# One matmul granule later for the first down product of an F part, and the projection's weights ahead of the last eight expert granules

## The reference

```python
def swiglu(v, wg, wu, wd):
    return (jax.nn.silu(v @ wg) * (v @ wu)) @ wd

def moe_swiglu(v, router, wg, wu, wd):
    ...
    y = jnp.zeros_like(v)
    for e in range(N_EXPERTS):                      # 8 experts, F = 2816
        y = y + combine[..., e:e + 1] * swiglu(v, wg[e], wu[e], wd[e])
    return y
...
    h = h + moe_swiglu(v, moe_router[j], moe_wg[j], moe_wu[j], moe_wd[j])
    ple_g = jax.nn.sigmoid((rmsnorm(h, norm_ple[i]) @ ple_gate[i]).astype(F32)).astype(h.dtype)
    h = h + ple_g * (p[i] @ ple_proj[i])
return rmsnorm(h, norm_final)
```

## Time and profile before

| | |
|---|---|
| median of 3 runs | 1570.85 us (1567.13 to 1571.53) |
| profiled execution, its own time | 1569.91 us |
| its span on the core | 1568.2 us |
| PE busy | 1537.9 us (98% of the span) |
| DVE, ACT, POOL busy | 600.8, 465.2, 63.2 us |
| read from HBM | 413.23 MB, 267 GB/s over the span |

### The profile page before, as it was taken

How to read it: one execution, slowest core, us unless ns; L and a number is a source line. 1 busy time by engine, 2 the same in 40 slices (tenths; PEclk the granted TensorE clock), 3 DMA queues, 4 the chain that set the end, 5 groups by cost and what they waited for, 6 DMA issues and landing times.

```text
span 1568.2 us, 33642 instructions
## 1 busy us (share of the span) xinstructions
PE 1537.9 (98%) x15282; PEld 1181.6 (75%) x15282; DVE 600.8 (38%) x831; ACT 465.2 (30%) x659; POOL 63.2 (4%) x101
## 2 busy tenths in 40 slices
PE   8999999999999999999999999999999999999987
PEld 7887888888888888788867677677766767777666
DVE  5787878555556777788210000000000000000025
ACT  5656434544455556434300000000000001000024
POOL 3100000000000100000000000000000000001001
PEclk9999999999999999999999999999999999999999
DMA  8445446565555445454999999999999999999940
GB/s 294 145 151 162 157 140 195 188 193 188 188 189 170 146 160 163 135 183 168 364 354 393 394 353 409 344 408 382 372 407 341 409 355 394 394 357 409 396 145 28
DMA packets 163396, 420.31 MB, mean 268 GB/s; under 512 B 16818, under 2 KB 42212, under 8 KB 163252
## 3 DMA queue, kind: packets, MB, share of 16 engines
q1 hardware_dynamic: 159168, 407.69, 71.6%
q0 software_dynamic: 2432, 8.65, 1.6%
q10 hardware_dynamic: 1652, 1.80, 0.4%
HBM read 413.23 MB, written 4.85 MB: 267 GB/s over the span
## 4 chain that ended last, share of the span: by engine, by line
PE 97%; ACT 1%; DVE 1%; DMA 0%; POOL 0%; issue 0%; SPq 0%; POOLq 0%; ACTq 0%; DVEq 0%
PE ps L2018 42%; PE ps L1561 15%; PE ps L1563 14%; PE ps L1562 14%; PE ps L2059 2%; PE ps L1660 1%; PE ps L2085 1%; PE ps L1621 1%; PE ps L1807 1%; PE ps L1670 1%; ACT ffT_area L634 1%; DMA arena<-in_w_in 0%; PE ps L2088 0%; PE ps L2095 0%; PE ps L2009 0%; PE ps L1831 0%
## 5 line engine op out<-in xcount | busy, mean ns | idle before, releaser
L1561 PE MATMUL ps<-whi,ahi 128*128 128x512 f32 (+1 forms) x984 | 391.2, 398 | 4.6 <-DVE wlo L982 3.0
L1563 PE MATMUL ps<-wlo,ahi 128*128 128x512 f32 (+1 forms) x984 | 383.2, 389 | 0.0
L1562 PE MATMUL ps<-whi,alo 128*128 128x512 f32 (+1 forms) x984 | 382.6, 389 | 0.0
L982 DVE TENSOR_TENSOR wlo<-arena,whi 128x1024 fp32r<-128x1024 f32 (+1 forms) x246 | 289.0, 1217 | 83.9 <-ACT whi L634 83.0
L634 ACT ACTIVATE whi<-arena 128x1024 fp32r<-128x1024 f32 (+1 forms) x246 | 245.6, 1053 | 99.9 <-PE ps L1563 89.1
L1476 DVE TENSOR_TENSOR ff_area<-ff_area,ps 128x768 f32<-128x768 f32 x24 | 22.9, 954 | 642.4 <-PE ps L2018 642.4
L2018 PE MATMUL ps<-arena 128*32 128x512 f32 (+3 forms) x3816 | 267.1, 428 | 0.0
L2018 PEld LDWEIGHTS ps<-arena 128*32 128x32 f32 x3816 | 188.8, 110 | 63.7 <-issue 1.3
L1561 PEld LDWEIGHTS ps<-whi,ahi 128*128 128x128 f32 x984 | 184.9, 188 | 47.3 <-issue 9.0
L2018 PE MATMUL ps<-expert_ring,arena 128*32 128x256 f32 (+3 forms) x3096 | 217.1, 426 | 0.0
L1563 PEld LDWEIGHTS ps<-wlo,ahi 128*128 128x128 f32 x984 | 184.7, 188 | 38.9
(11 more groups left out here) (260 smaller groups left out, 920.0 us busy)
## 6 DMA issues: line engine op xcount, KB each, us to landing
arena<-in_w_in SPq DMA_DIRECT2D x112, 512.0 KB, 4.5
arena<-in_moe_wd SPq DMA_DIRECT2D x92, 512.0 KB, 7.5
expert_ring<-in_moe_wd SPq DMA_DIRECT2D x84, 512.0 KB, 7.5
arena<-in_moe_wu SPq DMA_DIRECT2D x76, 512.0 KB, 9.0
arena<-in_moe_wg SPq DMA_DIRECT2D x68, 512.0 KB, 8.5
expert_ring<-in_moe_wg SPq DMA_DIRECT2D x60, 512.0 KB, 8.3
expert_ring<-in_moe_wu SPq DMA_DIRECT2D x52, 512.0 KB, 9.9
arena<-in_moe_wu SPq DMA_DIRECT2D x36, 384.0 KB, 3.9
```

The source lines that it names most:

```text
L982: return V.tensor_tensor(dst, src, hi.bitcast(f32), ALU.subtract)
L1561: TE.matmul(o, ahi[:, sa], whi[:, sw], start=start, stop=False)
L1562: TE.matmul(o, alo[:, sa], whi[:, sw], start=False, stop=False)
L1563: return TE.matmul(o, ahi[:, sa], wlo[:, sw], start=False, stop=stop)
```

## The change

It has three parts. First, in the lists for parts 1 and 2, D0 and D4 stand one place later: behind g1.2 and g2.2. Second, the loads of ple0, ple1 and ple2 stand in SP's order ahead of those of the last eight expert granules (u2.1 to D10 of the last expert); these eight lie in `arena` alone, and since three of its seven slots now hold the ple weights, they share the other four. So `RING_DONE` falls to 272. Third, ACT and DVE split these three granules at the places of u2.2, u2.3 and D6 of the last expert, where before they did it at the end of the expert and, for the last one on DVE, after it.

```diff
@@ -55,9 +55,9 @@
-MOE_ORDER += [("gate", 1, 0), ("gate", 1, 1), ("down", 0, 0), ("gate", 1, 2), ("gate", 1, 3), ("down", 1, 0), ("up", 1, 0),
+MOE_ORDER += [("gate", 1, 0), ("gate", 1, 1), ("gate", 1, 2), ("down", 0, 0), ("gate", 1, 3), ("down", 1, 0), ("up", 1, 0),
               ("up", 1, 1), ("down", 2, 0), ("up", 1, 2), ("up", 1, 3), ("down", 3, 0)]
-MOE_ORDER += [("gate", 2, 0), ("gate", 2, 1), ("down", 4, 0), ("gate", 2, 2), ("gate", 2, 3), ("down", 5, 0), ("up", 2, 0),
+MOE_ORDER += [("gate", 2, 0), ("gate", 2, 1), ("gate", 2, 2), ("down", 4, 0), ("gate", 2, 3), ("down", 5, 0), ("up", 2, 0),
               ("up", 2, 1), ("up", 2, 2), ("up", 2, 3)]
@@ -76,14 +76,19 @@
-SLOT_OF = [FREED[m % len(FREED)] for m in range(N_MOE)]
-for part in range(5):
-    waiting = [m for m in range(len(SLOT_OF)) if SLOT_OF[m] < ARENA_SLOTS and SLOT_OF[m] not in SLOT_OF[m + 1:]]
-    SLOT_OF.append(SLOT_OF[waiting[0]])
-BEFORE = [max([k for k in range(m) if SLOT_OF[k] == SLOT_OF[m]], default=None) for m in range(len(SLOT_OF))]
-USE = [sum(SLOT_OF[k] == SLOT_OF[m] for k in range(m)) for m in range(len(SLOT_OF))]
-RING_DONE = max(m for m in range(N_MOE) if SLOT_OF[m] >= ARENA_SLOTS) + 1
-OVER_SLOT = [slot for slot in range(ARENA_SLOTS) if slot not in SLOT_OF[N_MOE:]][0]
+TAIL = 8
+LOADS = list(range(N_MOE - TAIL)) + [N_MOE + i for i in range(3)] + list(range(N_MOE - TAIL, N_MOE)) + [N_MOE + 3, N_MOE + 4]
+SLOT_OF, BEFORE, USE, held = {}, {}, {}, {slot: [] for slot in FREED}
+for at, m in enumerate(LOADS):
+    if at < len(FREED):
+        slot = FREED[at]
+    else:
+        free = [slot for slot in FREED if held[slot][-1] < N_MOE and (slot < ARENA_SLOTS or m < N_MOE - TAIL)]
+        slot = min(free, key=lambda slot: held[slot][-1])
+    SLOT_OF[m], USE[m], BEFORE[m] = slot, len(held[slot]), held[slot][-1] if held[slot] else None
+    held[slot].append(m)
+RING_DONE = N_MOE - TAIL
+OVER_SLOT = [slot for slot in range(ARENA_SLOTS) if held[slot][-1] < N_MOE][0]
@@ -471,7 +476,7 @@ (SP)
-            for m in range(N_MOE + 5):
+            for m in LOADS:
@@ -922,8 +927,8 @@ (ACT)
-                            if e == NE - 1 and k >= PER_E - WR:
-                                convert(n + WR)
+                            if e == NE - 1 and PER_E - 7 <= k < PER_E - 4:
+                                convert(M0 + N_MOE + k - (PER_E - 7))
@@ -1474,10 +1479,10 @@ (DVE)
-                            if e == NE - 1 and k >= PER_E - 2:
-                                convert(n - 1 + WR)
-                                if k == PER_E - 1:
-                                    add_last_expert()
+                            if e == NE - 1 and PER_E - 7 <= k < PER_E - 4:
+                                convert(M0 + N_MOE + k - (PER_E - 7))
+                            if e == NE - 1 and k == PER_E - 1:
+                                add_last_expert()
@@ -1510,8 +1515,6 @@ (DVE)
-                if layer == 1:
-                    convert(first - 1 + WR)
```

## The result

| | before | after |
|---|---|---|
| first comparison, median | 1569.09 us (4 runs, 1567.13 to 1571.53) | 1556.07 us (4 runs, 1552.4 to 2243.31) |
| ratio | | 0.9907, 95% interval 0.9884 to 0.9931 |
| the same kernel again, median | 1570.92 us (11 runs) | 1553.34 us (4 runs, 1551.52 to 1555.93) |
| ratio | | 0.9893, 0.9878 to 0.9907 |
| profiled execution, its own time | 1569.91 us | 1555.45 us |

The change gains about 1%, and both intervals lie clear of 1. The execution of 2243.31 us ran at a mean granted clock of 0.653 where the others had 0.993 to 0.996; it is not in the ratio, but it counts in the median of the table, which is 1555.45 us without it.

A forecast was written before the change was run, and what follows sets the result against it. PE was taken as the bound, with its waits and clock deciding. Gains of 10.6 + 4.6 + 2.7 + 0.4 = 18.3 us, with loads costing 0, gave 1552 us (ratio 0.988), range 1549 to 1557.5.

The forecast's parts named there:

- What bounds the kernel: In the experts PE is the bound, and the transfers run ahead of it by up to 13 slots.
- Part 1: Experts: D0 and D4 one place later removes 16 waits of 0.66 us each: 10.6 us, bounds 9.3 and 10.9.
- The 1.94 us that the text took for g1.2: Experts: time of g1.2 or g2.2 behind the turn, covering ACT's copy, which fits into 0.58 us.
- Part 2 and the clock: End of last expert: wait for y's copy goes, 4.6 us; full clock saves 2.7 in combination, 0.4 in projection's first product.
- The loads: Last eight granules in four slots: about 2 us to spare at D6 and D7, cost 0, upper bound 3.9 us.
- 4.2 + 0.8 = 5.0 us for D6: Last expert: landing plus issue of D6's pair of transfers, against 7.8 us from slot release to use.
- The sum: Whole kernel: 10.6 + 4.6 + 2.7 + 0.4 = 18.3 us gained, giving 1552 us, ratio 0.988.
- a low clock in the combination: Rival, end of experts: the combination's clock is low all the same; gain 15.2 to 15.5 us, 1555 us; chance 0.08.
- The four slots: Rival, last expert: slots become a bound, up to 3.9 us waiting at D6 or D7; 1554 to 1559 us; chance 0.12.
- The wait didn't move: Rival, experts: D0's wait is for something longer than g1.2, so part 1 gives nothing; 1562.5 us; chance 0.03.
- The transfers didn't become the bound: Rival, expert stage: memory can't give 378 GB/s, PE waits at landings; a loss below 369 GB/s; chance 0.02.
- The limit of about 358 GB/s: HBM limit for a core; by it the expert stage takes 780 us and the kernel about 1594.

The follow-up runs named there:

- The list alone: Kernel before with only the two `MOE_ORDER` lines changed (D0 and D4 one place later), loads and splits as before: 1561.39 us, ratio 0.9933.
- The kernel with the busy wait: Kernel before with the new `MOE_ORDER` lines, plus 36 filler transposes on PE ahead of its wait for the copy of y: 1558.13 us, ratio 0.9918.
- three slots: Changed kernel with slot 1 barred to the last eight expert granules: 1557.87 us in one execution.
- two slots: Changed kernel with slots 0 and 1 barred to the last eight expert granules: 1561.49 us in one execution.

## Why the prediction was right, step by step

**What bounds the kernel.** PE, as read: with the named waits gone it is busy for every microsecond of the experts (the window below).

**Part 1: 10.6 us predicted.** From the first expert granule to the end of D10 it was 747.86 us and is 737.51: 10.35 us, within the bounds of 9.3 and 10.9. By the period of an expert a place gave 0.65 us and not 0.66. The reading of the start-to-start gap, and not of the idle time alone, was right: 16 times 0.58 would have been 9.3. The rows say where the rest comes from: without a wait the next granule starts 0.47 us after the start of a turn of 0.55, so the two overlap by 0.08, and a wait loses that too. The 1.94 us that the text took for g1.2 holds for g2.2 alone; g1.2 takes 2.60 (1077.77 to 1080.37), so the cover was larger than it said. The list alone shows the term by itself.

**Part 2 and the clock: 4.6 + 2.7 + 0.4 = 7.7 us predicted.** From the end of D10 to the end of the span it was 49.47 us and is 41.93: 7.54 us. The kernel with the busy wait separates it into 4.6 for the wait and 2.9 for the clock, where the text had 3.1 for the combination and the projection's first product together. The kernel that copies y first adds what the text didn't ask: the same gain was to be had from the order of the two streams alone.

**The loads: 0 predicted.** Right, but by a smaller margin. The step "4.2 + 0.8 = 5.0 us for D6" was mis-sized: a pair takes 6.2 us there, so there are some 1.3 us to spare (estimated above) and not the 2 that it gave in general and 2.8 for D6. The estimate came from the nearest row of a quiet queue, whose transfers belong to another tensor; the truth lay between it and the 10.9 of the earlier trace rows. That 10.9 is the median of its group, so it was no upper bound either.

**The sum: 18.3 us predicted.** The touched stages gave 17.9. Between profiled executions with the same clock ahead of the experts the difference is 18.4 us, between the medians of the second comparison 17.6, and between those of the first 13.6 (1569.09 less 1555.45). What the text lacked is the scatter ahead of the experts: it took the profiled execution as it was, and that one had full clock at the start and the shorter stretch at the router. The medians of the changed kernel (1553.34 and 1555.45) lie 1.3 and 3.5 us above the forecast of 1552.0, inside the range. That the second median comes as near as 1.3 us is partly luck, since the executions of one kernel scatter by 4 us and more; what bears the forecast out are the stages, 17.9 against 18.3. The forecast ratio of 0.988 lies inside the interval of the second comparison and just below that of the first.

**The rivals.** The gain given for a low clock in the combination should read 15.2 to 15.6 us (10.6 + 4.6 + 0.4), which changes nothing. The four slots didn't become a bound, but three do, with 2.6 us: the rival's mechanism is real and one slot away. The clock wasn't low in the combination, and the row-wise quarter products run at 1.00 (2.87 us for the 48). The wait didn't move to anything else. The transfers didn't become the bound; the window over the stage:

```profile
774.00:1511.80 737.80, 737.80 (x10585) 523.54 (x10584) 47.70 (x86) 61.81 (x100) 19.86 (x27) 1.00 0.99 377
```

PE is busy for all of it, at 377 GB/s where 378 was worked out. The limit of about 358 GB/s for a core that the prediction took from the Trainium skill (DMA: Bandwidth & Descriptors, "Specifications") doesn't bind this kernel, which uses one core; the same page, in "Bandwidth", says that it is the share of a core when both cores of an HBM domain stream, and that one alone gets more. The trace agrees with that as far as it goes: 377 GB/s over the stage; what the other core of the domain did isn't recorded. The prediction should have cited the two together.

## What to carry to other kernels

When a wait sits behind a producer of fixed length, put one piece of independent work between; read its price from start to start, since the gap is longer than the idle time. When an engine waits for a short instruction of another engine, look at what stands ahead of that instruction in its stream before moving loads: putting the copies of y ahead of the splits gave here all that a new slot plan gave. And price a stop of some microseconds of PE with the slower clock behind it: 4.6 us of waiting cost 7.5.

## What the runs showed of the hardware that wasn't expected

**The clock differs between executions of the same instructions.** Behind PE's wait of 2.2 to 3.6 us at the start it fell in seven of ten profiles, and not in the other three, whose waits (2.5, 2.5 and 3.0 us) lie among those of the seven (2.2 to 3.6 us). In the experts it didn't fall behind waits of 2.4 us (three slots) and 2.7 us (two slots), while it did behind the 4.56 us at the end. A low stretch costs some 2 us, both together 3.4. The executions of the changed kernel spread over 4.4 us and those of the list alone over 7.4 us, so the two stretches needn't be the whole of the scatter. What decides it in an execution stays open.

**Filler transposes do hold the clock.** 36 transposes of the identity in a wait of 4.6 us kept it at 1.00, where it stood at 0.50 behind an idle wait. At the router, where it was still low at the first of the 16 fillers, it came back during them or in the first few products of the gather (in others, the one before the change among them, it was back ahead of them: 1.95 us for the 16). With 4, in one profile, it stayed at 0.50 through 32 further products.

**A pair of 512 KB transfers took 6.2 us from issue to use at the end of the last expert,** twice, with PE waiting for it and one other pair close by. For single transfers issued in the middle of the stage the slowest group had a median of 10.9 us to landing, and the earlier trace rows had given 4.2.
